# Second attention over three steps a pair; both output projections in two halves of their sum

## The chip, the cores and the metric

The kernel runs on one NeuronCore of a Trainium2 chip. TensorE multiplies, VectorE and ScalarE work element by element, GpSimd makes part of the weights, and SyncE issues the weight transfers. The metric is the device time of one execution in microseconds. What follows is the source that was handed to the compiler, and one profiled execution of it.

## The reference, cut to what matters

A network of three layers on a sequence of 512 tokens, width 1024, all in float32. Two parts are touched. The first layer's attention has 8 heads of two score maps each, and its output goes through `a_w_o` (1024 x 1024). The second layer's has 16 heads with a part without position (128 wide) and a rotary part (64 wide, one key shared by all heads), and its output goes through `b_w_o` (2048 x 1024):

```python
sc = (jnp.einsum('bqhd,bkhd->bhqk', qn, k_nope)
      + jnp.einsum('bqhr,bkr->bhqk', qp, k_pe)).astype(jnp.float32) * scale
sc = jnp.where(causal_mask(i, s), sc, NEG_INF)
a = jax.nn.softmax(sc, axis=-1)
return jnp.einsum('bhqk,bkhv->bqhv', a.astype(v.dtype), v)
...
return o.reshape(b, s, MLA_HEADS * MLA_V_DIM) @ w_o
```

After each attention comes `h = h + mix`, then a feed-forward part on the normed `h`, then a per-layer embedding.

## The kernel before

**Layout.** Activations lie transposed: 1024 features are 8 chunks (DC) of 128 partitions by 512 tokens (S). A linear layer makes its output in tiles of 128 features by 512 tokens. Each tile is a sum over the input chunks, and each chunk takes three matmuls (lines 443 to 445, or 459 to 461 in `first_tile`): weights and inputs are split in a rounded high part and a low part, and high x high, high x low, low x high are added. Tiles alternate between the two banks of `lin`.

**Weights.** `STREAM` lists all weight groups in the order of use; in the parts touched here one group is one tile's weights (8 blocks of 128 columns, 512 KB), save for `b_pair`, whose pairs come in groups of 12 and 8 blocks. The slots form a ring of three. SyncE issues group n once the tile of group n-3 is done; ScalarE's `high_half(n)` makes the rounded part (line 1601); GpSimd subtracts for the low part (line 1988); only then can TensorE use it. ScalarE issues `high_half(n + 2)` at a written place, `before(n)`.

**Order.** Every engine runs a list that is written out by hand, with semaphore waits between engines. Nothing is reordered.

**First attention** (`a_step`). Step s projects head s (three `lin_` tiles), scores head s-1, and normalises the output of head s-2 (`tail`). Steps 8 and 9 (AH, AH + 1) have no projections: step 8 is the attention of the last head alone, step 9 the tail of its output. Then `out_highs` and `out_lows` split the 8 output chunks, and `output_products("a_wo", ...)` with `residual` makes 8 tiles of 8 blocks, adds each to `h`, and rounds it for the next layer (`rounding`, `add_square`, `remainder`: lines 912, 934, 918).

**Second attention** (`b_step`). Step s projects pair s: three tiles of queries, two of keys, two of values (`lin_(0)` to `lin_(6)`), with five sums of squares on TensorE (`sums`, line 719), and a rotation (line 729). The same step does the whole attention of pair s-1, head after head: `score(x, k)` for head x and query block 3-k (line 687 for the 128 wide part, line 689 for the 64 wide part), `biased` (VectorE, negative maximum too, line 1304), `exps` (ScalarE, 1816), `weights_` (VectorE, 1316), `turn_` (TensorE transposes, 536), `turned` (ScalarE copies out of `turn`, 1835), `product(x)` (TensorE, 710) and `output(x)` (VectorE, 1332). Both heads share the buffer `b_pt`. The bank of `scores` and of `turn` is chosen by k. Step 8 is the attention of the last pair alone. After it the last chunks are split, and `b_wo` runs as 16 half tiles of 8 blocks (`_halves`), two to an output chunk, each added to `h` by itself.

## Time and profile before

| what | us |
|---|---|
| median of 3 runs | 2546.3 (2545.51 to 2553.78) |
| profiled execution, its own time | 2546.92 |
| its span, first to last instruction | 2545.1 |
| TensorE busy in the span | 2369.6 (93%) |
| VectorE, ScalarE, GpSimd busy | 1179.0, 918.3, 832.9 |

An engine's busy time is the sum of its instructions. Overlapping ones are counted once. The profile's other views used here are the timeline (instructions in order of time), the waits (who waited for whom) and the stretches (busy time between two times).

### The profile page before, as it was taken

How to read it: one execution, taken by the hardware profiler on the slowest of the kernel's cores; microseconds unless marked ns; L12 is line 12 of the kernel's file. 1: busy time of each engine (PE TensorE's matmuls, PEld its weight loads, DVE VectorE, ACT ScalarE, POOL GpSimd, SP SyncE). 2: the span in 40 equal slices, each digit the busy share in tenths (PEclk: the TensorE clock that was granted, in tenths of full speed). 3: DMA queues.
4: the chain of work that ended last, by engine and by line, in shares of the span. 5: the costliest groups of instructions: out<-in, count | busy, mean ns of one | idle time of the engine just before them, and what ended most of it. 6: DMA issues, size and time to landing. Idle time of an engine off the chain costs nothing.

```text
span 2545.1 us, 25959 instructions
## 1 busy us (share of the span) xinstructions
PE 2369.6 (93%) x10172; PEld 1801.5 (71%) x10172; DVE 1179.0 (46%) x2151; ACT 918.3 (36%) x1458; POOL 832.9 (33%) x320
## 2 busy tenths in 40 slices
PE   6989899999998888988999999999898889999997
PEld 4666688887776555555888878777784468888876
DVE  5444565562265444454365551256516653333224
ACT  4454443332243344443243332231315533222223
POOL 2222244444333111111444443434320024444432
PEclk9999999999999899999999999999957979999998
DMA  7111133332222001001233232225220012333222
GB/s 248 52 57 50 58 92 99 95 105 91 88 93 66 33 30 33 30 25 33 92 99 97 94 104 91 88 94 163 83 67 1 1 50 91 99 100 101 91 97 76
DMA packets 57194, 201.02 MB, mean 79 GB/s; under 512 B 6288, under 2 KB 9888, under 8 KB 57072
## 3 DMA queue, kind: packets, MB, share of 16 engines
q1 hardware_dynamic: 54208, 194.94, 24.0%
q10 hardware_dynamic: 2864, 4.40, 0.5%
q8 instruction: 82, 1.34, 0.2%
q14 instruction: 40, 0.33, 0.0%
HBM read 197.19 MB, written 7.38 MB: 80 GB/s over the span
## 4 chain that ended last, share of the span: by engine, by line
PE 83%; DVE 7%; ACT 5%; issue 2%; DMA 2%; SPq 0%; POOL 0%; ACTq 0%; DVEq 0%; PEldq 0%
PE lin L443 22%; PE lin L445 22%; PE lin L444 22%; PE lin L758 2%; PE obank L710 2%; PE scores L689 1%; PE scores L687 1%; PE turn L536 1%; PE stat L719 1%; PE obank L607 1%; PE scores L830 1%; PE lin L459 1%; PE lin L460 1%; PE lin L461 1%; DMA slots<-in_w_a_qkv 1%
## 5 line engine op out<-in xcount | busy, mean ns | idle before, releaser
L1988 POOL TENSOR_TENSOR w_lo<-slots,w_hi 128x1024 fp32r<-128x1024 f32 (+3 forms) x314 | 830.4, 2645 | 1558.6 <-ACT w_hi L1601 1558.6
L1601 ACT ACTIVATE w_hi<-slots 128x1024 fp32r<-128x1024 f32 (+3 forms) x314 | 356.0, 1134 | 734.5 <-DMA slots<-in_w_ffn_in 281.0
L443 PE MATMUL lin<-g_hi,w_hi 128*128 128x512 f32 x1416 | 561.5, 397 | 7.5 <-DVE arena L1083 6.9
L444 PE MATMUL lin<-g_lo,w_hi 128*128 128x512 f32 x1416 | 552.3, 390 | 0.0
L445 PE MATMUL lin<-g_hi,w_lo 128*128 128x512 f32 x1416 | 552.3, 390 | 0.0
L443 PEld LDWEIGHTS lin<-g_hi,w_hi 128*128 128x128 f32 x1416 | 266.6, 188 | 78.1 <-issue 22.4
L444 PEld LDWEIGHTS lin<-g_lo,w_hi 128*128 128x128 f32 x1416 | 266.8, 188 | 58.6 <-issue 4.1
L445 PEld LDWEIGHTS lin<-g_hi,w_lo 128*128 128x128 f32 x1416 | 266.6, 188 | 56.1
L980 DVE TENSOR_TENSOR h<-lin,h 128x512 f32<-128x512 f32 x80 | 55.3, 691 | 384.3 <-PE lin L445 381.2
L443 PE MATMUL lin<-f_hi,w_hi 128*128 128x512 f32 x528 | 209.4, 397 | 4.3 <-DVE f_lo L1024 4.3
L445 PE MATMUL lin<-f_hi,w_lo 128*128 128x512 f32 x528 | 209.0, 396 | 0.0
L444 PE MATMUL lin<-f_lo,w_hi 128*128 128x512 f32 x528 | 208.9, 396 | 0.0
L443 PEld LDWEIGHTS lin<-f_hi,w_hi 128*128 128x128 f32 x528 | 99.6, 189 | 29.0 <-DVE f_lo L1024 5.1
L1663 ACT ACTIVATE arena<-arena,vec 128x512 f32<-128x512 f32 x88 | 71.8, 816 | 128.8 <-DVE arena L1039 128.8
L445 PEld LDWEIGHTS lin<-f_hi,w_lo 128*128 128x128 f32 x528 | 99.5, 188 | 24.0
L444 PEld LDWEIGHTS lin<-f_lo,w_hi 128*128 128x128 f32 x528 | 99.7, 189 | 23.7
L1621 ACT ACTIVATE arena<-h 128x512 f32<-128x512 f32 x72 | 45.2, 628 | 189.8 <-DVE arena L934 146.2
L1042 DVE SCALAR_TENSOR_TENSOR arena<-arena,vec 128x512 f32<-128x512 f32 x88 | 74.2, 844 | 79.2 <-ACT arena L1663 79.2
L1039 DVE TENSOR_TENSOR arena<-lin,r 128x512 f32<-128x512 f32 x88 | 60.8, 691 | 107.1 <-PE lin L445 106.8
L443 PE MATMUL lin<-c_mix_hi,w_hi 128*128 128x512 f32 x176 | 70.5, 400 | 2.8 <-POOL w_lo L1988 2.8
L1045 DVE SCALAR_TENSOR_TENSOR arena<-arena,vec 128x512 f32<-128x512 f32 x88 | 70.2, 798 | 3.1
L445 PE MATMUL lin<-c_mix_hi,w_lo 128*128 128x512 f32 x176 | 69.4, 394 | 0.0
(384 smaller groups left out, 3541.4 us busy)
## 6 DMA issues: line engine op xcount, KB each, us to landing
slots<-in_w_ffn_in SPq DMA_DIRECT2D x132, 512.0 KB, 3.5
slots<-in_w_ffn_out SPq DMA_DIRECT2D x48, 704.0 KB, 4.0
slots<-in_w_ple SPq DMA_DIRECT2D x24, 640.0 KB, 3.9
slots<-in_w_a_qkv SPq DMA_DIRECT2D x24, 512.0 KB, 3.5
slots<-in_w_c_in SPq DMA_DIRECT2D x23, 512.0 KB, 3.5
slots<-in_w_b_wo SPq DMA_DIRECT2D x16, 512.0 KB, 3.5
slots<-in_w_b_pair SPq DMA_DIRECT2D x8, 768.0 KB, 4.2
slots<-in_w_a_wo SPq DMA_DIRECT2D x8, 512.0 KB, 3.4
```

The costliest lines, as they stand in the source:

```text
L443: pe.matmul(lin[:, parity, :], hi, x_hi, start=k == 0, stop=False)
L444: pe.matmul(lin[:, parity, :], hi, x_lo, start=False, stop=False)
L445: mm = pe.matmul(lin[:, parity, :], lo, x_hi, start=False, stop=k == len(rhs) - 1)
L710: mm = pe.matmul(obank[:, j * P:S], b_v[:, 1 - par, x, j * P:(j + 1) * P], b_pt[:, j, j * P:S], start=j == 0, stop=j == NQ - 1)
L758: mm = pe.matmul(lin[:, t % 2, 0:2 * NCMP], w[x][:, c * P:(c + 1) * P].bitcast(F32), c_zp[:, k // 4, 8 * (k % 2) + c, :], start=c == 0 and ...
L980: ve.tensor_tensor(h[:, 2 * i + k, :], lin[:, (t + j) % 2, :], h[:, 2 * i + k, :], ALU.add)\
L1039: ve.tensor_tensor(f_u[:, k, 2:S + 2], lin[:, (t0 + k) % 2, :], r[:, :], ALU.mult)\
L1042: ve.scalar_tensor_tensor(out=f_c[:, k, :], in0=f_u[:, k, 1:S + 1], scalar=vec[:, w + 1:w + 2], in1=f_c[:, k, :], op0=ALU.mult, op1=ALU.ad ...
L1045: ve.scalar_tensor_tensor(out=f_c[:, k, :], in0=f_u[:, k, 0:S], scalar=vec[:, w:w + 1], in1=f_c[:, k, :], op0=ALU.mult, op1=ALU.add).then_ ...
L1601: ac.activation(w_hi[:, slot, at_], slots[:, slot, at_], ACT.Copy).then_inc(q.hi_made, 1)
L1663: ac.activation(f_c[:, k, :], f_u[:, k, 2:S + 2], ACT.Identity, bias=vec[:, w + 3:w + 4], scale=vec[:, w + 2:w + 3]).then_inc(q.f_first, 1)
L1988: po.tensor_tensor(w_lo[:, slot, at_], slots[:, slot, at_], w_hi[:, slot, at_].bitcast(F32), ALU.subtract).then_inc(q.weights_split, 1)
```

## The change

Second attention: a pair now takes three steps. Step s projects pair s, scores pair s-1, and does the last of the transposes and both products of pair s-2 (`late`). `score(k)` treats both heads at once: the two 128 wide matmuls, then the two 64 wide ones, head 0 on rows 0 to 63 and head 1 on rows 64 to 127, each head in its own bank of `scores`. Each head has its own bank of `turn` and its own buffer in `b_pts`. There is one step more, and steps 8 and 9 are without projections.

Output projections: `a_wo` becomes `a_wo0` and `a_wo1`, 8 groups of 4 blocks each, the first half of the sum over the input chunks (heads 0 to 3) and the second. `b_wo` becomes `b_wo0` and `b_wo1`, 8 groups of 8 blocks each (heads 0 to 7, then 8 to 15); before, the two halves of one output chunk followed each other. The 8 tiles of the first half (`early_output`, with `early_added` on VectorE) run inside steps 8 and 9 of their attention; the second half runs where all of it ran before. In the first attention, `out_highs` and `out_lows` of the heads move into the steps.

```diff
-    ("a_qkv", 3 * AH, (DC, DC), (1, 1)), ("a_wo", DC, (DC, DC), (1, 1)),
+    ("a_qkv", 3 * AH, (DC, DC), (1, 1)), ("a_wo0", DC, (4, 4), (1, 1)), ("a_wo1", DC, (4, 4), (1, 1)),
...
-    ("b_wo", 2 * DC, (BH // 2, BH // 2), (1, 1)),
+    ("b_wo0", DC, (BH // 2, BH // 2), (1, 1)), ("b_wo1", DC, (BH // 2, BH // 2), (1, 1)),
...
+def b_steps(step):
+    for s in range(B_PAIRS + 2):
+        step(s, s % 2, s < B_PAIRS, 1 <= s <= B_PAIRS, s >= 2)
...
+        b_o_hi = area_r("b_o_hi", at, BH, S); b_o_lo = area_r("b_o_lo", 0, BH, S)
...
+        b_pts = (low[:, 4:8, :], area(54 * S, NQ, S))
...
+    def early_output(name, m, rhs, n):
+        t = TILE[name] + m
+        tile(t, t % 2, weights(name, m), 0, rhs, (q.out_split, n + 1) if m == 0 else None)
...
+        def early(*ms):
+            if tail and not proj:
+                for m in ms:
+                    early_output("a_wo0", m, parts(a_o_hi, a_o_lo, 4), 0)
...
+        early(*((6,) if last else (0,)))
...
         score(1)
         lin_(1)
+        early(*((7,) if last else (1,)))
         score(2)
         sums(0)
+        if attn:
+            early(2)
         score(3)
         sums(1)
+        if attn:
+            early(3)
...
+                if k % 2:
+                    early(4 + k // 2)
...
+                wait(pe, q.b_biased, 8 * (s - 1) + 2 * k)
                 qb = slice(i * P, (i + 1) * P)
+                for x in range(2):
+                    pe.matmul(scores[:, x, 0:LEN[i]], b_qn[:, 1 - par, x, qb], b_kn[:, 1 - par, x, 0:LEN[i]],
+                              start=True, stop=False)
+                for x in range(2):
+                    rows = slice(64 * x, 64 * x + 64)
+                    pe.matmul(scores[:, x, 0:LEN[i]], b_qp[rows, 1 - par, qb], b_kp[rows, 0:LEN[i]],
+                              start=False, stop=True).then_inc(q.b_scored, 1)
...
+            if late:
+                pair = s - 2
+                pe.wait_ge(q.b_tcopied, 8 * pair + 7 + x)
+                pe.wait_ge(q.b_rope, min(s, B_PAIRS))
+                wait(pe, q.b_otaken, 2 * pair + x)
                 for j in range(NQ):
+                    mm = pe.matmul(obank[:, j * P:S], b_v[:, par, x, j * P:(j + 1) * P],
+                                   b_pts[x][:, j, j * P:S], start=j == 0, stop=j == NQ - 1)
                 mm.then_inc(q.b_pv, 1)
...
+                early_output("b_wo0", m, parts(b_o_hi, b_o_lo, BH // 2), DC)
+        if not proj and attn:
+            score(0); turn_(3, s - 2, late); early(0); product(0); score(1); product(1); early(1); score(2)
+            turn_(0); early(2); score(3); turn_(1); early(3); turn_(2); early(4)
+            return
+        if not proj:
+            turn_(3, s - 2, late); early(5); product(0); early(6); product(1); early(7)
+            return
+        lin_(0); score(0); turn_(3, s - 2, late); lin_(1); product(0); lin_(2); sums(0); score(1); product(1)
+        lin_(3); sums(1); lin_(4); score(2); sums(2); turn_(0); lin_(5); sums(3)
         if proj:
             pe.wait_ge(q.b_normed, 5 * s + 3)
+            wait(pe, q.b_otaken, 2 * s - 2)
             pe.matmul(obank[:, :], rot, b_rt[:, 0, :], start=True, stop=True).then_inc(q.b_rotated, 1)
+        score(3); turn_(1); lin_(6); sums(4); turn_(2)
...
+    def early_added(name, *ms):
+        for m in ms:
+            t = TILE[name] + m
+            ve.wait_ge(q.tile_done, t + 1)
+            ve.tensor_tensor(h[:, m, :], lin[:, t % 2, :], h[:, m, :], ALU.add).then_inc(q.tile_taken, 1)
...
+        if last:
+            early(6)
         if tail:
             ve.wait_ge(q.a_ofactor, s - 1)
             ve.scalar_tensor_tensor(out=a_o[:, s - 2, :], in0=a_rawo, scalar=asub, in1=a_ri[:, 2, :],
                                     op0=ALU.mult, op1=ALU.mult).then_inc(q.a_onormed, 1)
+        if last:
+            early(7)
+        if attn and tail:
+            out_lows(0, a_o, a_o_hi, a_o_lo, {5: (0, 1), 6: (2, 3), 7: (4,), 8: (5,)}.get(s, ()))
...
         take_(1)
         if isinstance(s, int) and s == 0:
             angles()
+        if attn:
+            early(0)
         biased(2)
         weights_(1)
+        if attn:
+            early(1)
         biased(3)
         normed(0)
         weights_(2)
+        if attn:
+            early(2)
         weights_(3)
         normed(1)
+        if attn:
+            early(3, 4, 5)
...
+        lows = lambda *chunks: out_lows(DC, b_o, b_o_hi, b_o_lo, chunks)
+        early = lambda *ms: early_added("b_wo0", *ms)
+        if not proj and attn:
+            biased(0); lows(*range(BH // 2)); weights_(0); output(0); biased(1); output(1); weights_(1); early(0)
+            biased(2); weights_(2); early(1); biased(3); weights_(3); early(2)
+            return
+        if not proj:
+            early(3); lows(*range(BH // 2, BH - 2)); early(4); output(0); early(5); output(1); lows(BH - 2, BH - 1)
+            early(6, 7)
+            return
+        take_(0); biased(0); take_(1); take_(2); output(0); weights_(0); biased(1); normed(0); take_(3); normed(1)
+        output(1); weights_(1); take_(4); biased(2); normed(2); take_(5); normed(3)
...
+        weights_(2); biased(3); take_(6); normed(4); weights_(3)
...
+                before(GROUP["a_wo0"] + m)
+        last = not attn and tail
+        if last:
+            early(5)
...
+        if last:
+            early(6)
+        if s >= 3:
+            ac.wait_ge(q.a_onormed, s - 2)
+            out_highs(a_o, a_o_hi, (s - 3,))
         exps(1)
+        if attn:
+            early(0)
...
+        early = lambda m: before(GROUP["b_wo0"] + m)
+        if not proj and attn:
+            highs(0, 1, 2); turned(3, s - 2, late); exps(0); highs(*range(3, BH // 2)); early(0); exps(1); exps(2)
+            turned(0); early(1); exps(3); turned(1); early(2); highs(*range(BH // 2, BH - 2)); turned(2); early(3)
+            return
+        if not proj:
+            turned(3, s - 2, late); early(4); early(5); early(6); highs(BH - 2, BH - 1); early(7)
+            return
+        squared(0); exps(0); turned(3, s - 2, late); squared(1); squared(2); split(0); factor_(0); exps(1); squared(3)
+        factor_(1); squared(4); exps(2); factor_(2); turned(0); factor_(3); exps(3); turned(1); factor_(4); split(1)
+        turned(2)
```

## Rows read from the trace of the kernel before

**Rows 1.** Page, busy time of each engine, share, instructions

```profile
PE 2369.6 (93%) x10172; PEld 1801.5 (71%) x10172; DVE 1179.0 (46%) x2151; ACT 918.3 (36%) x1458; POOL 832.9 (33%) x320
```

**Rows 2.** Stretches: us, busy of PE, PEld, DVE, ACT, POOL, granted clock, DMA

```profile
261.50:281.20 19.70, 12.29 (x38) 6.21 (x38) 11.06 (x38) 12.41 (x31) 0.00 (x0) 0.74 0.01 1
1063.00:1105.20 42.20, 37.06 (x148) 22.36 (x146) 20.49 (x48) 19.33 (x41) 5.99 (x2) 1.00 0.08 26
```

**Rows 3.** Waits of TensorE from 829.7 to 1149.5: total us, times, longest

```profile
PE stat L719 <- ACT arena L1645: 13.3, 7, 2.1
PE turn L536 <- DVE g L1316: 13.1, 7, 1.9
PE obank L729 <- DVE arena L1332: 6.1, 7, 0.9
```

**Rows 4.** Timeline of TensorE, second attention: start, duration, what

```profile
829.69 0.80 PE L443 MATMUL lin<-b_cq_hi,w_hi 128*128 128x512 f32 x1
1061.48 0.48 PE L443 MATMUL lin<-b_cq_hi,w_hi 128*128 128x512 f32 x1
1065.31 1.12 PE L689 MATMUL scores<-arena 64*128 64x512 f32 x2
1066.36 0.50 PE L443 MATMUL lin<-b_cq_hi,w_hi 128*128 128x512 f32 x1
1078.62 0.48 PE L689 MATMUL scores<-arena 64*128 64x128 f32 x2
1103.01 2.42 PE L710 MATMUL obank<-low 128*128 128x512 f32 x8 [0.37 <-ACT low L1835]
1105.19 0.48 PE L443 MATMUL lin<-b_cq_hi,w_hi 128*128 128x512 f32 x1
1145.52 4.12 PE L710 MATMUL obank<-low 128*128 128x512 f32 x8 [0.37 <-ACT low L1835]
1149.47 1.02 PE L687 MATMUL scores<-arena 128*128 128x512 f32 x2
```

**Rows 5.** Timeline of TensorE, a score of the first attention and its successor

```profile
231.51 1.13 PE L563 MATMUL scores<-arena 64*128 64x512 f32 x4
232.56 0.50 PE L443 MATMUL lin<-g_hi,w_hi 128*128 128x512 f32 x1
```

**Rows 6.** Timeline of GpSimd and VectorE in a step of the second attention

```profile
1076.73 3.47 POOL L1988 TENSOR_TENSOR w_lo<-slots,w_hi 128x1536 fp32r<-128x1536 f32 x1 [23.64 <-ACT w_hi L1601]
1077.92 2.82 DVE L1325 SCALAR_TENSOR_TENSOR arena<-arena,vec 128x512 f32<-128x512 f32 x1 [1.12 <-ACT arena L1647]
1098.58 0.69 DVE L1340 TENSOR_TENSOR arena<-obank,sinb 128x512 f32<-128x512 f32 x1 [1.28 <-PE obank L729]
1100.52 0.28 DVE L1304 CUSTOM_DVE_ANT_0 g<-scores,consts 128x128 f32<-128x128 f32 x1
```

**Rows 7.** Timeline of VectorE: output splits, and adds of two output tiles in succession

```profile
1173.54 11.89 DVE L966 TENSOR_TENSOR b_o_lo<-arena,b_o_hi 128x512 fp32r<-128x512 f32 x16
1265.73 0.69 DVE L980 TENSOR_TENSOR h<-lin,h 128x512 f32<-128x512 f32 x1 [2.67 <-PE lin L445]
1271.33 0.69 DVE L980 TENSOR_TENSOR h<-lin,h 128x512 f32<-128x512 f32 x1 [4.91 <-PE lin L445]
```

**Rows 8.** Timeline of VectorE, one output chunk of the first projection, and TensorE's next layer

```profile
304.16 0.69 DVE L980 TENSOR_TENSOR h<-lin,h 128x512 f32<-128x512 f32 x1 [2.69 <-PE lin L445]
306.46 0.74 DVE L918 SCALAR_TENSOR_TENSOR g_lo<-h,vec,g_hi 128x512 fp32r<-128x512 f32 x1
331.76 1.02 PE L427 MATMUL stat<-arena,consts 128*128 128x512 f32 x2
```

**Rows 9.** GpSimd by form: count, busy us, mean ns

```profile
L1988 POOL TENSOR_TENSOR w_lo<-slots,w_hi 128x1024 fp32r<-128x1024 f32 x234 | 574.7, 2457 | 1090.0 <-ACT w_hi L1601 1090.0
```

**Rows 10.** Timeline of ScalarE: the rounded part of a group of 8 blocks

```profile
1094.46 1.04 ACT L1601 ACTIVATE w_hi<-slots 128x1024 fp32r<-128x1024 f32 x1
```

**Rows 11.** Page, transfers: count, KB each, us from issue to landing

```profile
slots<-in_w_b_wo SPq DMA_DIRECT2D x16, 512.0 KB, 3.5
```

More of the change, by code:

```diff
@@ L1202, in normed, with early @@
                                                 op0=ALU.mult, op1=ALU.mult).then_inc(q.a_normed, 1)
+                def early(*ms):
+                    if tail and not proj:
+                        early_added("a_wo0", *ms)
+                last = not attn and tail
                 biased(0)
@@ L1343, in b_step @@
                     ve.tensor_tensor(b_qp[:, par, :], b_rt[:, 1, :], b_rt[:, 2, :], ALU.add).then_inc(q.b_rope, 1)
-                biased(1, 3); weights_(1, 2); weights_(1, 3); output(1)
-            b_steps(ve, b_step)
-            out_lows(DC, b_o, b_o_hi, b_o_lo, range(BH))
-            residual("b_wo", "ffn1", "ffn1", g_hi, g_lo, q.h_gained)
+                weights_(2); biased(3); take_(6); normed(4); weights_(3)
+            b_steps(b_step)
+            residual("b_wo1", "ffn1", "ffn1", g_hi, g_lo, q.h_gained)
             add_square("ffn1", DC - 1)
@@ L1736, in factor_, with early @@
                         inv_sqrt(a_ri[:, j, :], AQK, q.a_summed, q.a_logged, q.a_factor, 2 * s + j + 1, 2 * s + j + 1)
+                def early(m):
+                    if tail and not proj:
+                        before(GROUP["a_wo0"] + m)
+                last = not attn and tail
+                if last:
+                    early(5)
                 if tail:
@@ L1752, in a_step @@
                 factor_(0)
+                if attn:
+                    early(1)
                 exps(3)
                 factor_(1)
+                if attn:
+                    early(2)
                 if proj:
@@ L2005, in _halves, with _two @@
     return tiles.reshape(n, P, 2, k // 2).transpose(0, 2, 1, 3).reshape(2 * n, P, k // 2)
+def _two(tiles):
+    k = tiles.shape[2] // 2
+    return tiles[:, :, :k], tiles[:, :, k:]
 def _columns(v):
```

184 lines of the change are left out of this document (74 added, 110 removed).

## The prediction

> **What bounds the kernel now.** I read the page's busy times first: TensorE is busy for 2369.6 of 2545.1 us, the others less than half of it [rows 1]. So the change can only give back two things: TensorE's waits and slow stretches, and TensorE's own work. The stretches show where those are [rows 2]. The first attention's last step and tail, 261.5 to 281.2, keeps TensorE busy for 12.29 of 19.70 us at a granted clock of 0.74, part of it at the lower level, 1.2 GHz. In the second attention it is busy 37.06 of 42.20 us of a step. The waits name the causes: over seven steps, 13.3 us for ScalarE's logarithm before a sum of squares, 13.1 us for VectorE's weights before the last transposes, 6.1 us for the output copy before the rotation [rows 3], and 0.37 us a step for the copies ahead of the second product [rows 4]. That is 5.0 us a step.
>
> **Second attention, TensorE's work in a step.** One step runs from 1061.48 to 1105.19, 43.7 us [rows 4]. Four waits take 5.2 us of it by name (the first sum waited 2.0 here). Each costs some 0.2 more, since a matmul that isn't waited for starts before the one ahead has ended: the product that starts at 1103.01 lasts 2.42 but its successor starts after 2.18 [rows 4]. That leaves 37.7 us of work. The change touches one piece of it. The 64 wide part of a score at 512 columns takes 1.05 us from start to start (1065.31 to 1066.36), and 0.48 less an overlap of 0.07 at 128 [rows 4]; with 0.84 and 0.62 for the sizes between, by a straight line, that is 2.9 us a head. It uses half the rows of the array. The first attention has just such matmuls in pairs, one head on each half of the rows and in its own bank: the pair at 512 columns takes 231.51 to 232.56, also 1.05 us, for two [rows 5]. `score(k)` now puts both heads' 64 wide matmuls side by side, so a pair pays 2.9 instead of 5.8 us. Bounds: 0 if they don't overlap, 2.9 if they do as in the row; I take 2.9, the row being of the same shape. Work in a step: 34.8 us.
>
> **Second attention, the waits of a step.** I laid the new order out with durations of the step from 1061.48, time 0 being the start of `lin_(0)`. `score(0)` starts at 2.9, `product(0)` at 9.0, `score(1)` at 15.0, `product(1)` at 17.3, `score(2)` at 23.4, `turn_(0)` at 26.0, the rotation at 29.3, `score(3)` at 30.2, `turn_(1)` at 31.3, `lin_(6)` at 32.0, `turn_(2)` at 34.3. What each needs: `product(0)` needs copies that end by 8.3, the first sum a square of 3.5, the rotation `normed(2)`, made at 28.6 after a factor at 27.9. The three old waits are covered by tiles and products of another pair. The late one is `turn_(2)`. VectorE does the rotary terms when the rotation has ended, 1.94 us to the next `biased` (1098.58 to 1100.52 [rows 6]), from 31.2 on since `normed(3)` is ahead. With `weights_(2)`, 0.9, and two `biased` of 128, 0.6, it is at 34.7; ScalarE's two exponentials and two copies end at 36.1. So `turn_(2)` stands 1.6 us, and behind it the whole next step. A step is 34.8 + 1.6 = 36.4 us. It could be 34.8 if that chain is faster, and 40 if the wait on VectorE that the next sentences tell of lands on it.
>
> In the row VectorE's `normed` took 2.82 us, beside 0.75 when alone, and ended 0.5 us after GpSimd's subtraction of 3.47 us [rows 6]. Laid out, the large subtraction now lies at 16.7 to 20.2 and meets `normed(0)`, the small one at 2.0 to 4.5 of the next step and meets `weights_(3)`. Their users, `lin_(3)`'s take at 21 and `turn_(3)` at 5.8, come later, so I count nothing; if both were on the path, it would be 2.1 us twice a step. The Trainium skill (SBUF, State Buffer, "Who interferes with whom") says that a VectorE instruction with two inputs in SBUF and a reading GpSimd one exclude each other, and that the later one blocks fully. By that rule the meeting costs what is left of the subtraction, up to 3.5 us; the trace's 2.1 agrees, and this order makes two meetings a step where I counted one.
>
> **Second attention, the sum.** Before, steps 1 to 7 go from 829.69 to 1149.47, 319.8 us [rows 4]; the two products before the next start took 4.1 us instead of 2.4 in places, the lower clock after a wait. After, step 1 has no products of an earlier pair (2 x 2.2) nor `turn_(3)` (0.3): 31.7. With six of 36.4, 250.1. Gain 69.7.
>
> From 1149.47 to the last output tile (1271.33 [rows 7]) there are 121.9 us before. After, TensorE has, in steps 8 and 9 and the second half: 17.7 of pair 7's attention (the two heads' shares of 43.7 us, counted by start to start), less 2.9, plus 4.7 of pair 6, and 16 tiles of 5.6 us (1265.73 to 1271.33 [rows 7]), 89.6: 109.1. Waits added: `score(0)` no longer has a tile ahead of it and stands until `normed(4)` of step 7, 1.8. The first early tile needs 8 chunks split: VectorE starts its lows behind `biased(0)`, ScalarE's highs stand behind the last copies and exponentials, so chunk 0 is there 1.8 us after TensorE asks and the last at 11.9; a low is 0.74 us (11.89 / 16 [rows 7]) against 0.7 for a chunk's matmuls, so it keeps pace and costs 2.1 altogether. The ring: a group of 512 KB takes 3.5 us to land [rows 11], 1.04 on ScalarE [rows 10] and 2.46 on GpSimd [rows 9], 7 us against two tiles ahead, 11.2; ScalarE's `early(m)` stands behind its `exps`, at the latest 2 us before its group is needed. Sum 113.0, gain 8.9.
>
> **First attention.** In steps 2 to 7, a high (0.53) and lows (up to 1.4) are put where ScalarE and VectorE wait for tiles; I take 0, bounds 0 and 1 a step. From 261.5 on, before: the last step and tail, then 8 tiles of 5.57 us, then the next layer's first tile, which ends at 331.76 [rows 8]. After: eight tiles of 2.8 us (12 matmuls) go between scores. VectorE now has `early` adds of 0.7 ahead of `biased` and `weights_`, and ScalarE its highs of weights behind `exps(1)` to `exps(3)`. Laid out: `early(2)` at 273.2 (waits 2.1, its low part is made late), `early(3)` 276.5, the product at 286.9, `early(7)` ends at 295.7; VectorE stands in `out_lows` for ScalarE's high behind the tail's factor, so head 7's low is ready at 298.9 and the first tile of the second half ends at 299.6. The other seven would end at 319.2 by TensorE. VectorE has 3.04 us a chunk (304.16 to the end of 306.46's [rows 8]) against 2.8, so its last remainder is at 323.3, and the next layer's first tile, which starts meanwhile, ends at 324.0. Gain 7.8. A group of 256 KB isn't in the trace. With the 3.5 us of one of twice its size as the upper end and 0 as the lower, landing, ScalarE and GpSimd take 5.3 at most (3.5, 0.53 and 1.23, the latter two by half of [rows 9, 10]), against 5.6 for two tiles: near the bound. If it paces the 16 tiles, each is at most 0.5 us later: 8 us.
>
> **Sum.** 69.7 + 8.9 + 7.8 = 86.4 us. Layouts by hand leave out small waits; I choose 0.5 us for each of eight steps, 4.4 with rounding, and take 82. The profiled execution's 2546.9 (span 2545.1 and 1.8 around it) less 82 is 2464.9; the median of the runs shown is 0.6 lower: 2464.
>
> **Rivals.**
> - The 64 wide pairs run one after the other. For it: between them and the 128 wide ones the array changes its use of rows, and here they add to banks just written. Against: [rows 5]. 8 x 2.9 = 23 us of gain lost: 2487. Chance 0.07.
> - The step becomes bound by the chain of VectorE and ScalarE, `normed`, rotary terms, `biased(3)`, `exps(3)`, `turned(1)`, with a GpSimd subtraction on it. For: it ends 1.3 us after TensorE already, and 2.82 against 0.75 in [rows 6]. Against: the subtractions lie elsewhere in the layout. 40 us a step, 7 x 3.6 = 25: 2489. Chance 0.13. It is also what the skill's rule would give if both meetings lay on the chain (29 us, 2493).
> - The ring paces the small groups: 2472, inside the likeliest's range. Chance 0.05.
> - Slower than before: TensorE falls to 1.2 GHz in the second attention. For: the clock fell behind short waits there, a product of 4.12 us where another took 2.42 [rows 4], and the new order has one wait in each step. Against: fewer waits, and 1.00 granted in a whole step that has four [rows 2]. Full speed work of eight steps is some 278 us; at the lower level it costs as much again. From 82 us of it at that level, three tenths, the gain is gone; with half of it there, 57 us over before: 2603. Chance 0.04.
>
> **Numbers.** Likeliest 0.71, 2464, its own range 2452 to 2480. Range 2450 to 2493: it takes in the first three rivals and an order that flows better than laid out. What a measurement can tell from no change is 0.3%, some 8 us; the likeliest and three rivals lie far under it. Faster 0.93, within 0.3% 0.02, slower 0.05.
>
> **What would show it.** In the profile after: steps of the second attention of 36 to 37 us between first tiles; the 64 wide scores in pairs with a start-to-start of 1.05; no wait on the logarithm or ahead of the rotation; a wait of 1 to 2 us at the third transposes; the stretch from the last projecting step to the last tile of `b_wo1` of 113 us; the first attention's last steps followed by tiles 3.0 us apart. It is wrong if the steps are above 40 us, if the early tiles wait for `w_lo`, or if the granted clock there falls.

## The result, and the profile after

| | before | changed |
|---|---|---|
| median, us | 2548.6 (2545.5 to 2553.8, 4 runs) | 2481.0 (2479.0 to 2483.1, 4 runs) |
| span of the profiled execution, us | 2545.1 | 2477.2 |

The ratio is 0.9733, with a 95% interval of 0.9712 to 0.9754: faster, 2481 us where 2464 was forecast, inside the range.

The page of the changed kernel, busy time of each engine; it answers to [rows 1]:

```profile
PE 2325.4 (94%) x10172; PEld 1788.4 (72%) x10172; DVE 1199.3 (48%) x2159; ACT 914.5 (37%) x1466; POOL 834.1 (34%) x328
```

TensorE has as many instructions as before and 44 us less busy time; the other 24 of the 68 us that the span lost were idle time. Where they went is read from the same three marks in both traces. The first row is the start of step 1 of the second attention, the second the first score of step 8, the third the add of `b_wo1`'s last tile (TensorE, TensorE and VectorE of the changed kernel; start, duration, what, and in brackets what it waited for):

```profile
829.97 0.79 PE L439 MATMUL lin<-b_cq_hi,w_hi 128*128 128x512 f32 x1
1089.80 2.94 PE L701 MATMUL scores<-arena 128*128 128x512 f32 x4 [1.53 <-DVE arena L1377]
1203.48 0.69 DVE L1011 TENSOR_TENSOR h<-lin,h 128x512 f32<-128x512 f32 x1 [2.47 <-PE lin L441]
```

Before, they stood at 829.69, 1149.47 and 1271.33 [rows 4, 7]. The 1.53 us in brackets belong to the last part, so step 7 ends at 1088.3:

| stretch | before | forecast | after | gained | forecast |
|---|---|---|---|---|---|
| all up to step 1, first attention and its projection in it | 829.7 | 821.9 | 830.0 | -0.3 | 7.8 |
| steps 1 to 7 | 319.8 | 250.1 | 258.3 | 61.5 | 69.7 |
| step 8 to `b_wo1`'s last tile | 121.9 | 113.0 | 115.2 | 6.7 | 8.9 |
| sum | | | | 67.9 | 86.4, less 4.4 allowed |

The stretches of the changed kernel: the first attention's last step and tail, step 1, a steady step, and step 8 to the end of `b_wo1` (us; busy and count of TensorE, its weight loads, VectorE, ScalarE, GpSimd; granted clock; DMA share, GB/s). They answer to [rows 2]:

```profile
261.13:290.50 29.37, 27.34 (x122) 19.63 (x122) 14.94 (x42) 12.67 (x31) 7.72 (x6) 1.00 0.21 54
829.90:864.60 34.70, 30.37 (x135) 19.69 (x134) 20.25 (x46) 18.21 (x38) 5.87 (x2) 1.00 0.16 54
864.60:901.85 37.25, 34.48 (x154) 22.53 (x154) 22.33 (x49) 18.70 (x42) 5.86 (x2) 1.00 0.11 37
1088.00:1203.30 115.30, 112.05 (x473) 85.37 (x473) 52.33 (x91) 39.64 (x70) 39.63 (x17) 0.97 0.22 69
```

In this execution the first attention's tail runs at a granted clock of 1.00, where it was 0.74 [rows 2], with early tiles in it, and yet nothing is gained up to step 1. In e9, the same kernel, it is 0.94 there; what comes of that is told under e2. In a steady step TensorE has 34.5 us of work in 37.25 us. TensorE's waits from 830 to 1088 in the changed kernel (total us, times, longest), against [rows 3]:

```profile
PE turn L536 <- ACT low L1907: 11.0, 7, 1.6
PE stat L732 <- ACT arena L1704: 8.1, 8, 1.9
PE obank L751 <- DVE arena L1377: 1.8, 7, 0.3
```

And TensorE's rows of a steady step, against [rows 4]: two scores with the `turn_` after them, the three waits, and the next step's score.

```profile
867.50 1.88 PE L701 MATMUL scores<-arena 128*128 128x512 f32 x4
869.31 1.13 PE L705 MATMUL scores<-arena 64*128 64x512 f32 x4
870.37 0.33 PE L536 MATMUL turn<-consts,g 128*128 128x128 f32 x1
893.32 1.10 PE L732 MATMUL stat<-arena,consts 128*128 128x512 f32 x2 [0.94 <-ACT arena L1704]
894.67 1.12 PE L751 MATMUL obank<-arena,consts 128*128 128x512 f32 x2 [0.26 <-DVE arena L1377]
901.32 0.79 PE L536 MATMUL turn<-consts,g 128*128 128x128 f32 x4 [1.57 <-ACT low L1907]
904.73 0.59 PE L701 MATMUL scores<-arena 128*128 128x512 f32 x1
```

The step is 904.73 - 867.50 = 37.23 us, and it comes out of the rows: 34.48 of work, 1.57, 0.94 and 0.26 of waits. The 64 wide part of both heads takes 1.06 us from start to start, as for one head before (1.05 [rows 4]). The wait of 1.57 at `turn_(2)` is the 1.6 that was laid out. The one of 0.94 at the fourth sum was not foreseen, nor was 1.93 at the same place in step 1 (with 0.57 ahead of the third sum there):

```profile
856.08 1.10 PE L732 MATMUL stat<-arena,consts 128*128 128x512 f32 x2 [1.93 <-ACT arena L1704]
```

`normed(0)` was seen beside it, blocked by GpSimd's subtraction in every step (GpSimd and VectorE, changed kernel):

```profile
881.37 3.47 POOL L2070 TENSOR_TENSOR w_lo<-slots,w_hi 128x1536 fp32r<-128x1536 f32 x1 [12.40 <-ACT w_hi L1660]
882.57 2.83 DVE L1377 SCALAR_TENSOR_TENSOR arena<-arena,vec 128x512 f32<-128x512 f32 x1
903.82 2.39 POOL L2070 TENSOR_TENSOR w_lo<-slots,w_hi 128x1024 fp32r<-128x1024 f32 x1 [18.98 <-ACT w_hi L1660]
904.08 2.21 DVE L1368 TENSOR_SCALAR g<-g,small 128x128 f32<-128x128 f32 x1
```

After the first attention the chunks of the second half were to come 3.04 us apart. They come 2.73, 2.82, 3.18, three times 3.49 to 3.50, and 4.48 apart. One chunk of the 3.5 us kind, with ScalarE and GpSimd beside VectorE (changed kernel), against [rows 8]:

```profile
307.74 0.63 ACT L1680 ACTIVATE arena<-h 128x512 f32<-128x512 f32 x1 [2.34 <-DVE arena L956]
308.27 0.61 ACT L1660 ACTIVATE w_hi<-slots 128x512 fp32r<-128x512 f32 x1
308.96 1.30 POOL L2070 TENSOR_TENSOR w_lo<-slots,w_hi 128x512 fp32r<-128x512 f32 x1 [2.20 <-ACT w_hi L1660]
308.23 0.68 DVE L1011 TENSOR_TENSOR h<-lin,h 128x512 f32<-128x512 f32 x1
308.94 1.60 DVE L934 TENSOR_SCALAR g_hi<-h,vec 128x512 fp32r<-128x512 f32 x1
...
311.73 0.68 DVE L1011 TENSOR_TENSOR h<-lin,h 128x512 f32<-128x512 f32 x1
```

The rounding on L934 takes 1.60 us; where no subtraction runs (300.23) it takes 0.49. The seven after the first take 1.40, 1.27, 1.60, 1.59, 1.59, 0.49 and 1.88; behind the one of 0.49, the remainder (L940) takes 2.84 instead of 0.75, beside the larger subtraction of the next layer's weights. The loop keeps it so: L956 releases ScalarE's square, behind which stands the high half of the next weights, and that releases the subtraction just when VectorE comes to the next rounding. At the end TensorE waits for the next layer's first weights and then runs its first matmuls at the lower clock level (0.63 instead of 0.39 us each, seven of them):

```profile
319.88 5.62 POOL L2070 TENSOR_TENSOR w_lo<-slots,w_hi 128x1024 fp32r<-128x1024 f32 x2 [2.63 <-ACT w_hi L1660]
322.77 0.79 PE L455 MATMUL lin<-g_hi,w_hi 128*128 128x512 f32 x1 [2.40 <-POOL w_lo L2070]
...
324.21 0.63 PE L455 MATMUL lin<-g_hi,w_hi 128*128 128x512 f32 x1
...
329.90 1.02 PE L423 MATMUL stat<-arena,consts 128*128 128x512 f32 x2
```

The sum of squares behind that tile (L423) starts at 329.90, and this is the mark for the tile's end here: 1.9 us before its old place [rows 8], 5.9 after the forecast one.

### The profile page after: what moved, and what is told of

Its sections match the earlier page's. It is cut to its first block, busy times and chain, and to the rows that moved or that the text cites. A ratio compares the mean times of both kernels' runs of the same rounds, so it can differ in the third digit from the quotient of the medians.

```text
span 2477.2 us, 26002 instructions
## 1 busy us (share of the span) xinstructions
PE 2325.4 (94%) x10172; PEld 1788.4 (72%) x10172; DVE 1199.3 (48%) x2159; ACT 914.5 (37%) x1466; POOL 834.1 (34%) x328
## 4 chain that ended last, share of the span: by engine, by line
PE 81%; DVE 9%; ACT 6%; issue 2%; DMA 2%; SPq 0%; POOL 0%; ACTq 0%; DVEq 0%; PEldq 0%
PE lin L439 22%; PE lin L441 22%; PE lin L440 22%; PE lin L780 2%; DVE arena L1377 1%; PE scores L701 1%; PE obank L723 1%; PE turn L536 1%; ACT arena L1704 1%; PE lin L455 1%; PE obank L621 1%; PE lin L456 1%; PE lin L457 1%; PE scores L705 1%; PE scores L852 1%
## 5 line engine op out<-in xcount | busy, mean ns | idle before, releaser
L1011 DVE TENSOR_TENSOR h<-lin,h 128x512 f32<-128x512 f32 x72 | 49.7, 691 | 330.9 <-PE lin L441 323.1
L1073 DVE SCALAR_TENSOR_TENSOR arena<-arena,vec 128x512 f32<-128x512 f32 x88 | 73.5, 836 | 79.1 <-ACT arena L1722 79.1
L1377 DVE SCALAR_TENSOR_TENSOR arena<-arena,vec 128x512 f32<-128x512 f32 x40 | 45.2, 1130 | 58.3 <-ACT arena L1706 58.3
L439 PE MATMUL lin<-c_mix_hi,w_hi 128*128 128x512 f32 x176 | 70.4, 400 | 3.1 <-POOL w_lo L2070 3.1
L1076 DVE SCALAR_TENSOR_TENSOR arena<-arena,vec 128x512 f32<-128x512 f32 x88 | 70.2, 798 | 3.1
```

Of the source, the lines that this page charges most:

```text
L439: pe.matmul(lin[:, parity, :], hi, x_hi, start=k == 0, stop=False)
L1011: ve.tensor_tensor(h[:, 2 * i + k, :], lin[:, (t + j) % 2, :], h[:, 2 * i + k, :], ALU.add)\
L1073: ve.scalar_tensor_tensor(out=f_c[:, k, :], in0=f_u[:, k, 1:S + 1], scalar=vec[:, w + 1:w + 2], in1=f_c[:, k, :], op0=ALU.mult, op1=ALU.ad ...
L1076: ve.scalar_tensor_tensor(out=f_c[:, k, :], in0=f_u[:, k, 0:S], scalar=vec[:, w:w + 1], in1=f_c[:, k, :], op0=ALU.mult, op1=ALU.add).then_ ...
L1377: ve.scalar_tensor_tensor(out=dst, in0=b_raw[:, j, :], scalar=v1(vname), in1=b_ri[:, j, :], op0=ALU.mult, op1=ALU.mult).then_inc(q.b_norme ...
```

## The experiments

Three groups of four kernels, each group on one chip with runs of the kernel before on the same chip. The changed kernel and e1, which turn out to be worth the same, differ by 0.002 in their ratios between two groups (5 us), so smaller differences across groups are not read, and the traces decide. Positions in a trace have a spread too: step 1 of the second attention starts at 829.97 us in the changed kernel's, and at 832.24, 832.98 and 834.93 in those of e9, e4 and e3, whose code is the same up to there. So small gains are read as stretches between two marks, not as positions.

**e1, only the second attention's part.** The first attention, its projection and `a_wo` are those of before, everything else is the changed kernel:

```
-    ... ("a_wo0", DC, (4, 4), (1, 1)), ("a_wo1", DC, (4, 4), (1, 1)),
+    ... ("a_wo", DC, (DC, DC), (1, 1)),
```

> The change in the second attention and its projection alone; the first attention and its projection as before. Theory (from the two traces: the first projection's part won 0.5 us by the middle of the next layer's end, the second's 68.3): 0.973 of the kernel before, within 3 us of the changed kernel, which was at 2481. Rival (the first part is worth what was forecast, 7.8 us, and something else in the second attention lost the missing time): some 8 us above the changed kernel, 2489.

Measured 2480.3 us, ratio 0.9711 (0.9693 to 0.9728). **e2, only the first attention's part:**

```
-    ("b_wo0", DC, (BH // 2, BH // 2), (1, 1)), ("b_wo1", DC, (BH // 2, BH // 2), (1, 1)),
+    ("b_wo", 2 * DC, (BH // 2, BH // 2), (1, 1)),
```

> The change in the first attention and its projection alone. Theory: 0 to 2 us under the kernel before (ratio 0.999 to 1.000), with tiles of the second half 3.5 us apart and a wait of 2.4 us for the low part of the next layer's first weights. Rival: 8 us under it (0.997) if the forecast's sum held and the loss lies elsewhere.

Measured 2552.7 us, ratio 1.0002 (0.9992 to 1.0011). The whole gain is the second attention's; the first part is worth nothing within 0.1%. Its trace holds the wait for an early tile's weights that the whole change has at the same place (2.03 there too), and the one for the last add of the early half (1.90):

```profile
275.43 0.50 PE L443 MATMUL lin<-a_o_hi,w_hi 128*128 128x512 f32 x1 [2.03 <-POOL w_lo L2053]
279.97 0.49 PE L569 MATMUL scores<-arena 64*128 64x128 f32 x4
```

The tile behind that wait takes 4.54 us here, up to the score. In the trace of the changed kernel it takes 2.98:

```profile
272.60 0.50 PE L439 MATMUL lin<-a_o_hi,w_hi 128*128 128x512 f32 x1 [2.03 <-POOL w_lo L2070]
275.58 0.49 PE L563 MATMUL scores<-arena 64*128 64x128 f32 x4
```

Where it takes 4.54, eight of its twelve matmuls have 0.60 to 0.63 us instead of 0.39, the lower clock level. Twelve kernels here have the early tiles of the first attention, and in each the wait is 2.02 or 2.03. Behind it, four traces have the tile of 2.98 (the changed kernel, e5, e8, e12) and eight the tile of 4.54, e9 among them, which is the changed kernel again. That decides what the first part is worth. Counted from step 8's first score in the first attention to the mark at the end of the next layer's first tile:

| trace | us |
|---|---|
| before, and e1, which has the old first part | 70.2, 70.2 |
| new first part, tile of 2.98 (changed kernel, e5) | 68.8, 68.9 |
| new first part, tile of 4.54 (e2, e3, e4, e6, e9, e10) | 70.4 to 70.5 |

So of the 1.9 us that the changed kernel's trace shows at this mark, 1.6 hang on the clock of one tile; with the tile of 4.54 nothing is won, and the medians of e2 say the same.

**e3, the heads not paired.** The second loop over the heads goes, so each head's 64 wide matmul follows its own 128 wide one:

```
                         for x in range(2):
                             pe.matmul(scores[:, x, 0:LEN[i]], b_qn[:, 1 - par, x, qb], b_kn[:, 1 - par, x, 0:LEN[i]],
                                       start=True, stop=False)
-                        for x in range(2):
                             rows = slice(64 * x, 64 * x + 64)
```

> The changed kernel, but in score(k) each head's 64 wide matmul follows its own 128 wide one, so the two 64 wide ones are no longer neighbours. All else equal. Theory: the pairs overlap in the changed kernel, so 8 x 2.9 = 23 us are lost again: 2504. A softer form: some of it is hidden in the wait of 1.6 us at the third transposes, which comes from a chain that starts before score(3) and would shrink by 0.4 a step: 2501. Rival (the matmuls don't overlap, the gain is from the waits alone): no change, 2481.

Measured 2501.9 us, ratio 0.9801 (0.9784 to 0.9817): 21.6 us over e1 on the same chip. The rows of a score of the unpaired kernel and the same score one step later:

```profile
873.66 1.02 PE L701 MATMUL scores<-arena 128*128 128x512 f32 x2
874.61 1.12 PE L704 MATMUL scores<-arena 64*128 64x512 f32 x2
875.66 1.12 PE L701 MATMUL scores<-arena 128*128 128x512 f32 x2
...
913.16 1.02 PE L701 MATMUL scores<-arena 128*128 128x512 f32 x2
```

Each 64 wide matmul costs 1.05 us alone, and a step is 39.50. TensorE's work in it is 38.15 us, 3.67 more than paired: the 2.9 of the forecast, and 0.8 more, since a 128 wide matmul of 512 columns takes 1.05 us to the next start with a 64 wide one ahead of it, and 0.9 behind another 128 wide one. The step grows by 2.27 only: with more work ahead of it, the wait at `turn_(2)` falls from 1.57 to 1.0 and the one at the fourth sum goes. Slower TensorE work partly fills the waits behind it. Of the 21.6 us, the traces show 14.8 between the first scores of steps 1 and 8 (271.4 against 256.6) and 5.4 behind them (120.6 against 115.2), part of that at the lower clock.

**e4, the first half of `b_wo` after the attention.** The eight early tiles move from between steps 8's and 9's scores and products to behind them, with their adds and with ScalarE's rounded parts of their weights (all but the first). TensorE's order:

```
-  score(0); turn_(3, s - 2, late); early(0); product(0); score(1); product(1); early(1); score(2)
-  turn_(0); early(2); score(3); turn_(1); early(3); turn_(2); early(4)
+  score(0); turn_(3, s - 2, late); product(0); score(1); product(1); score(2)
+  turn_(0); score(3); turn_(1); turn_(2)
...
+  turn_(3, s - 2, late); product(0); product(1); early(*range(8))
```

> The changed kernel, but the eight tiles of the first half of the second projection run after the last attention product, none inside steps 8 and 9. Theory: TensorE then stands in steps 8 and 9 for the chains of VectorE and ScalarE as it did in the last step before (4.3 us idle plus slow matmuls at the lower clock) and again before the first projection tile: 10 to 15 us above the changed kernel, 2491 to 2496. Rival (the projection tiles only moved, nothing was idle there): 2481 to 2484.

Measured 2495.3 us, ratio 0.9781 (0.9765 to 0.9797): 15 us over e1. The waits that the early tiles had covered, in the timeline of this kernel:

```profile
1105.75 4.61 PE L723 MATMUL obank<-arena,low 128*128 128x512 f32 x8 [4.79 <-DVE arena L1384]
...
1119.88 0.72 PE L536 MATMUL turn<-consts,g 128*128 128x128 f32 x2 [2.97 <-ACT low L1907]
```

With three short ones (0.22, 0.62 and 0.88) they sum to 9.5 us, and the product behind the longest takes 4.61 us where 2.42 is usual without a wait, as at the lower clock level. From step 8 to the last tile this kernel takes 126.8 us and e9 112.0, both with their first score at full speed. So it is the placing of the first half inside the last steps that is worth some 15 us.

**e5, the weights' high half earlier,** so that GpSimd's subtraction has ended before `normed(0)`. In ScalarE's order:

```
- ... squared(1); squared(2); split(0); factor_(0); ...
+ ... squared(1); split(0); squared(2); factor_(0); ...
```

> The changed kernel with one order on ScalarE: in a projecting step of the second attention split(0) (the rounded part of the 1536 column group, which releases GpSimd's subtraction of 3.5 us) stands ahead of squared(2) and not behind it, so the subtraction runs some 4 us earlier, while VectorE waits for tiles. Theory (VectorE's normed(0), 2.83 us instead of 0.75 behind the subtraction, makes the logarithm late that TensorE waits for at the fourth sum, 0.94 and 0.2 of refill a step, and 2.5 in step 1): normed(0) takes 0.75, the waits before the sums go, 8 us under the changed kernel, 2473. Rival (the logarithm is late by ScalarE's own order): no change within 2 us.

Measured 2473.6 us, ratio 0.9691 (0.9656 to 0.9726). In the trace the block is gone, and the fourth sum waits as before (VectorE's two `normed`, and TensorE, of this kernel):

```profile
916.20 0.75 DVE L1377 SCALAR_TENSOR_TENSOR arena<-arena,vec 128x512 f32<-128x512 f32 x1
921.62 0.75 DVE L1377 SCALAR_TENSOR_TENSOR arena<-arena,vec 128x512 f32<-128x512 f32 x1 [1.94 <-ACT arena L1706]
901.18 1.88 PE L701 MATMUL scores<-arena 128*128 128x512 f32 x4
926.99 1.10 PE L732 MATMUL stat<-arena,consts 128*128 128x512 f32 x2 [0.94 <-ACT arena L1704]
938.40 1.88 PE L701 MATMUL scores<-arena 128*128 128x512 f32 x4
```

The step is 37.22 as in the changed kernel. The theory that the blocked `normed(0)` causes the wait of 0.94 falls for the steady steps: `normed(1)` waits 1.94 us for its factor anyway, and the block disappears in that. So the median lies where the theory put it (2473) without the mechanism of the theory. Only step 1 is 0.9 us shorter (33.42 between its two first scores, 34.34 with the block). The profiled run's span is that of the changed kernel less 0.9 as well (2476.3, 2477.2). The median is lower by more than that; its interval overlaps that of the changed kernel, and the trace shows nothing for it.

**e6, the copies first.** `turned(1)` ahead of `exps(3)` on ScalarE:

```
- ... turned(0); factor_(3); exps(3); turned(1); factor_(4); split(1)
+ ... turned(0); factor_(3); turned(1); exps(3); factor_(4); split(1)
```

> The changed kernel with one order on ScalarE: turned(1) ahead of exps(3). The last transposes of a projecting step wait 1.57 us for these copies, which stand behind exponentials that wait for VectorE's rotary terms. Theory: the wait goes, 7 x 1.57 and 0.2 of refill each, 12 us under the changed kernel, 2469. Rival (the step is bound by the whole chain over VectorE, so that the wait only moves, to score(0) of the next step or to the sums): under 4 us.

Measured 2471.5 us, ratio 0.9682 (0.9644 to 0.9721). The theory holds: the wait at `turn_(2)` is gone and a step takes 35.48 us, 1.75 less; between the first scores of steps 1 and 8 it is 11.2 less. What is left of TensorE's waits from 869 to 1082, six steps, beside 0.26 a step ahead of the rotation:

```profile
PE stat L732 <- ACT arena L1704: 5.6, 6, 0.9
```

**e7, the first projection without its subtraction.** GpSimd subtracts 16 columns only, and TensorE takes the rounded part in place of the low part; this kernel leaves out the low part of the weights of `a_wo`'s second half:

```
+                if name == "a_wo1":
+                    return w_hi[:, n % RING, :], w_hi[:, n % RING, :]
...
+                if name == "a_wo1":
+                    at_ = slice(0, 16)
```

> The changed kernel, but for the eight groups of the second half of the first projection GpSimd subtracts 16 columns and not 512, and TensorE takes the rounded part in place of the low part (this leaves out the low part of those weights). Matmuls, transfers and VectorE's work are the same. Theory (GpSimd's 1.3 us and VectorE's rounding shut each other out, so rounding takes 1.6 instead of 0.5 and a chunk 3.49 us): tiles 2.8 to 2.9 us apart, 5 us less, and part of the wait of 2.4 for the next layer's first low part and of the slow matmuls behind it: 5 to 8 us under the changed kernel. Rival (the transfers of 256 KB pace the tiles): still 3.5 us apart, no change.

Measured 2476.5 us, ratio 0.9705 (0.967 to 0.9739). VectorE's timeline of this kernel:

```profile
308.37 0.69 DVE L1013 TENSOR_TENSOR h<-lin,h 128x512 f32<-128x512 f32 x1 [0.79 <-PE lin L443]
309.10 0.49 DVE L936 TENSOR_SCALAR g_hi<-h,vec 128x512 fp32r<-128x512 f32 x1
311.15 0.69 DVE L1013 TENSOR_TENSOR h<-lin,h 128x512 f32<-128x512 f32 x1 [0.31 <-PE lin L443]
```

The chunks come 2.79 us apart instead of up to 3.50, the rounding takes 0.49 again, and VectorE waits for TensorE: this was the subtraction, and no transfer paces these tiles. TensorE's wait for the next layer's weights stays, 2.0 us. From step 8's first score to the end of the next layer's first tile it is 66.1 us with an early tile of 4.54, 4.3 less than in the other traces with one.

**e8, the rounding on ScalarE.** For this norm ScalarE makes the rounded chunk, computing everything:

```
-                    if gain:
+                    if gain and gain != "ffn0":
...
+                    if norm == "ffn0":
+                        ac.wait_ge(q.tile_taken, t + c)
+                        ac.activation(g_hi[:, c, :], h[:, c, :], ACT.Identity, scale=v1(norm, c)).then_inc(q.h_rounded, 1)
```

> The changed kernel, but ScalarE makes the eight rounded chunks ahead of the first feed-forward part (line 934's work behind the first projection) and VectorE doesn't. GpSimd's subtractions stay. Theory: VectorE's time a chunk with two SBUF inputs falls to 0.68 + 0.75, and with GpSimd's 1.3 that is 2.7 us, under TensorE's 2.8: tiles about 3.0 apart, 3 to 6 us under the changed kernel. Rival (transfers pace them): no change. Rival (ScalarE, with 0.6 more a chunk ahead of its squares, becomes late): slower by 1 to 4 us.

Measured 2472.0 us, ratio 0.969 (0.9656 to 0.9724). ScalarE's rounded part of the next layer's first weights, and TensorE at its first tile, in this kernel:

```profile
317.30 1.06 ACT L1660 ACTIVATE w_hi<-slots 128x1024 fp32r<-128x1024 f32 x1 [1.41 <-DMA slots<-in_w_ffn_in]
320.87 0.50 PE L455 MATMUL lin<-g_hi,w_hi 128*128 128x512 f32 x1 [1.42 <-POOL w_lo L2073]
...
326.44 1.02 PE L423 MATMUL stat<-arena,consts 128*128 128x512 f32 x2
```

The chunks come 2.9 to 3.0 us apart, but for the last (4.50). The tile ends 3.5 us earlier than in the changed kernel, 65.3 us behind step 8's first score where that one has 68.8 (both with an early tile of 2.98), and no matmul of it is at the lower clock. Both rivals fall for the tiles. The median is 9 us lower, more than the trace shows for the change, and stands in another group. The first row is a limit that comes next: with ScalarE early, the rounded part of the next layer's weights waits 1.41 us for their transfer, and TensorE's wait of 1.42 hangs on it.

**e9, the changed kernel again,** for the chip of the next three.

> The changed kernel itself, to stand beside the next three on one chip. Earlier it took 2481.0 us (ratio 0.9733), and with only the second attention's part 2480.3. Expected by every theory: 2479 to 2483 us, ratio 0.972 to 0.974, a steady step of 37.2 us.

Measured 2479.4 us, ratio 0.9731 (0.971 to 0.9751), steady step 37.23.

**e10, the third logarithm ahead of the exponentials,** on top of e6:

```
- ... squared(4); exps(2); factor_(2); turned(0); factor_(3); turned(1); ...
+ ... squared(4); factor_(2); exps(2); turned(0); factor_(3); turned(1); ...
```

> Two moves in ScalarE's order, nothing else: turned(1) ahead of exps(3), as before (2471.5 us, steady step 35.48), and factor_(2) ahead of exps(2). Theory: the wait of 0.94 us a step at the fourth sum is for the logarithm of the third, which stands behind exps(2) (four instructions, 1.0 us) in ScalarE's order and not behind VectorE's locked normed(0). Then the wait goes and a steady step takes 34.5 to 34.7 us, seven of them 6 us less than with turned(1) alone: 2464 to 2467 us. Rival, that the wait is passed on from VectorE (the late normed(1) or biased blocks): the step stays at 35.5 us and the time at 2471. Second rival: exps(2), 1.3 us later, makes turn_(2) wait in its place, and the step stays between 35.2 and 35.6.

Measured 2472.8 us, ratio 0.9695 (0.9677 to 0.9713), as e6. TensorE's longest waits of this kernel in its six steady steps, 869 to 1082:

```profile
PE turn L536 <- DVE g L1368: 2.9, 6, 0.5
```

The theory named the cause and the second rival the outcome. The wait was for ScalarE's order: with `factor_(2)` ahead of `exps(2)` it is gone, 5.6 us of it. And nothing is gained: the step is 35.48 as in e6, since `turn_(2)` now waits, for VectorE's `weights_(2)` and not for ScalarE's copies; the next step's first tile starts 32.55 us into the step in e6 and 32.53 in e10. The two kernels' rows from the start of `score(0)` say why. In e6 (start at 905.10) and in e10 (start at 869.24) the fourth factor's `normed` begins at the same 28.68 us:

```profile
933.78 0.75 DVE L1377 SCALAR_TENSOR_TENSOR arena<-arena,vec 128x512 f32<-128x512 f32 x1 [0.86 <-ACT arena L1706]
937.03 0.35 DVE L1368 TENSOR_SCALAR g<-g,small 128x256 f32<-128x256 f32 x1
```

```profile
897.92 0.75 DVE L1377 SCALAR_TENSOR_TENSOR arena<-arena,vec 128x512 f32<-128x512 f32 x1 [1.83 <-ACT arena L1706]
901.16 0.35 DVE L1368 TENSOR_SCALAR g<-g,small 128x256 f32<-128x256 f32 x1
```

`normed(3)` needs everything that ScalarE does from `squared(4)` to `factor_(3)`, in whatever order, and it does it without a gap: 928.68 to 933.75 in e6, 892.83 to 897.89 in e10; VectorE's rotary terms and `weights_(2)` follow, which end 32.3 us into the step in both, and `turn_(2)` needs them.

**e11, e5, e6 and e8 together; e12, with e10's move as well.**

> The three single moves of before together: the weights' high half ahead of squared(2) (2473.6), turned(1) ahead of exps(3) (2471.5), the rounding after the first attention on ScalarE (2472.0). If their gains over the changed kernel (on its ratio 7 to 9 us each) add up: about 2457 us, ratio 0.964. If the split's gain was only in step 1 and the last steps (its steady step had stayed at 37.2): 2460 to 2463 us, ratio 0.966, steady step 35.4.

> The last kernel with factor_(2) ahead of exps(2) as well. By the theory that the third logarithm holds the fourth sum: steady step 34.5 to 34.7 us and 6 us less than the last kernel, about 2453 to 2457 us, ratio 0.963. By the rival that VectorE is behind it: same as the last kernel within 1 us.

Measured e11 2461.2 us, ratio 0.9647 (0.9628 to 0.9665), steady step 35.48, step 1 31.58 between its scores. e12 2462.2 us, ratio 0.9658 (0.964 to 0.9675), steady step 35.47. e11 is the fastest kernel, 18.2 us under the changed one on the same chip. Of the 15.2 us between the two spans (2476.0 and 2460.8), 12.1 lie between the first scores of steps 1 and 8: 2.7 in step 1, 1.75 in each of five, and 0.7 in the last, since step 8's first score now waits 2.67 us for `normed(4)` where it waited 1.53. For e11 the second of its two cases held (2460 to 2463), for e12 the rival.

## Why the prediction was right, and where it was off

**Right in mechanism and sign.** The 64 wide matmuls of the two heads overlap: work in a step fell to 34.5 us (34.8 forecast), and e3, which takes away the pairing alone, gives back 21.6 us; the rival that they don't overlap falls. The pairing is worth more than the 2.9 us a step that the forecast took: 3.7 of work (e3). The old waits on the logarithm, on VectorE's weights and ahead of the rotation went from 32.5 us in seven steps [rows 3] to 8.1, 0 and 1.8, and the wait of 1.6 us at `turn_(2)` for ScalarE's copies came where it was laid out. e6 shows that it was ScalarE's order alone. Two of the signs that the prediction named did not come: there is a wait on the logarithm and one ahead of the rotation, and the steps are 37.2 us, just outside 36 to 37. And by its last sentence it would be wrong if the early tiles wait for `w_lo`: one does, 2.03 us, which its own layout had as 2.1, so that sign contradicted the text that it closed.

**Steps 1 to 7, 8.2 us too little gained.** The term that was mis-sized is the waits of a step: 2.8 us instead of 1.6. "The three old waits are covered by tiles and products of another pair" failed for the sums: `factor_(2)` stands behind `exps(2)` on ScalarE, so the fourth sum stands 0.94 us (e10), and 0.26 was left ahead of the rotation. A steady step is 37.23 instead of 36.4, its work being 0.3 less: 5 us in six. Step 1 took 34.7 instead of 31.7, and that is 30.4 of work, the 1.6 that was forecast, 0.26 ahead of the rotation, and 2.5 ahead of the third and fourth sums. It has no products of an earlier pair, which in the other steps give the factors time; that I subtracted their work and not their cover is the likely error, argued from the order and shown by no run. 0.9 of the 2.5 is the blocked `normed(0)` (e5).

**"I count nothing" for VectorE's two meetings with the subtraction.** The places were right, both meetings came (2.83 us beside 0.75, 2.21 beside 0.29), and in a steady step the first costs nothing on the path (e5). Behind the second, `turn_(3)` starts without a wait (870.37 above); what the second costs VectorE's own chain no run here tests. In step 1 the first one did cost time, 0.9 us. The rule of the Trainium skill (SBUF, State Buffer, "Who interferes with whom"), by which the later instruction blocks fully, fits the first: `normed(0)` began 1.20 us after the subtraction's start and ended 0.56 after its end, not far from its own length of 0.75. By the starts in the records it does not fit the rounding after the first attention, which starts 0.02 us before the subtraction and was the one held. The rival that made a bound of it (40 us a step) falls with 37.2.

**Step 8 to the last tile, 2.2 us.** The waits that were named came, 1.53 at `score(0)` (1.8) and 1.73 at the first early tile (2.1). What was not counted is the clock behind them: the score block took 4.6 us and the first early tile 7.2, part of both at the lower level. In e9, the same kernel, they took 3.0 and 5.7, and the stretch 112.0 us, 1.0 under the 113.0 of the forecast. So this term was sized rightly for a full clock, and whether 3.2 us come on top differs from execution to execution. e4 shows that the early tiles are what hides this stretch's waits.

**First attention, nothing instead of 7.8.** Up to 299 us the layout held in the trace shown (`early(2)` waiting 2.03 for 2.1, the first tile of the second half ending at 299.5 for 299.6), and that was luck: in eight of twelve traces the tile behind that wait takes 1.6 us longer (e2). Three steps of the layout failed. The wait of 2.1 was priced as a wait, with nothing for the lower clock behind it. "VectorE has 3.04 us a chunk": the chunks came up to 3.50 and at the end 4.48 apart, because the roundings, and one remainder, stand under GpSimd's subtractions (e7: 2.79 without); the last remainder ended at 327.0 for 323.3. And "the next layer's first tile, which starts meanwhile, ends at 324.0": it started only at 322.77, since its weights' high half stands on ScalarE behind the squares, the subtraction follows at 319.88, and the clock fell in the wait. I had placed TensorE and VectorE and not the weights of the tile that comes next. The tile ends 5.9 us late, which leaves 1.9 of the gain in this trace and nothing in the traces with the longer early tile. The 2.1 us that the trace loses from there to step 1 need no instruction of their own: that stretch takes 497.9 us before and 497.2 to 500.1 in six traces with the same code in it (the changed kernel, e3, e4, e7, e8, e9). The rival that the ring of 256 KB groups paces the tiles had the right effect and the wrong cause: with the transfers as they were, e7's tiles follow each other by TensorE's own time.

**The sum.** 86.4 less 4.4 was forecast and 67.9 came: 8.2 short in the steps, 2.2 behind them, 8.1 in the first part, less the 4.4 that had been allowed, 14.1 together. The measured median is 16.7 above the forecast one: the changed kernel's profiled execution was its fastest, 2.0 under its median, and the old one's stood 0.6 above the median from which the forecast was taken. What was lost ahead of step 1 and behind step 7 is in part the clock of one execution; steps 1 to 7 take 258.3 us in e9 too. The slower rival never came near: 1.00 granted in all of steps 1 to 7.

## What to carry to other kernels

When work is reordered so that TensorE's waits are covered, list for every other engine what stands ahead of the instruction that TensorE will want next, its weight preparation included: here ScalarE's in-order list (a logarithm behind exponentials, copies behind exponentials, a next layer's weights behind squares) set the two longest waits of a step and the one ahead of the next layer, and moving one call (`turned(1)`) gave more than the whole first-attention part. A blocked instruction is on the path only if its user doesn't wait for something else that ends later; look for the second wait in the same row before pricing it. And when a wait goes and the time stays, compare the starts of the chain's instructions against the step's own start: equal offsets, as here, show the chain that sets the step. Before a term of 2 us is read from one trace, look for the same stretch in the others of the same code: here one tile takes 3.0 or 4.5 us by the clock behind its wait, and it made or unmade the gain of a whole part.

## What the runs showed of the hardware

- A rounding by a per-partition scale (VectorE, one SBUF input besides it, 128x512) takes 0.49 us alone and 1.60 beside a GpSimd subtraction of 1.30 us whose record starts 0.02 us after its own: by the records the earlier one was held, until 0.28 us after the subtraction's end. ScalarE releases that subtraction at one fixed point of VectorE's loop, and the two met in six chunks of eight (1.27 to 1.88 us).
- Two 64 wide matmuls of 512 columns on different halves of the rows take 1.06 us together and 1.05 each when a 128 wide one stands between them, also when they add to banks that 128 wide matmuls have just written. Alternating is dearer for the 128 wide ones as well: 1.05 us to the next start behind a 64 wide one, 0.9 behind another 128 wide one (e3 and the changed kernel).
- The wait's length alone doesn't decide whether matmuls at the lower clock level follow it. In front of the first score of step 8, a wait of 1.53 us was followed by a score of 2.94 us in the changed kernel and by one of 1.98 in its repetition (e9); a wait of 2.70 by one of 3.78 in e10, one of 2.68 by one of 1.98 in e6. After the first attention a wait of 2.02 or 2.03 us was followed by a tile of 2.98 us in four traces and of 4.54 in eight.
